# Two adaLN units weighed by GpSimd in attention in place of the even input stage, and the odd input stage's opening in another order

## Chip, cores and metric

One core of a Trainium2 chip runs the whole program. The time is device time in microseconds from the first to the last instruction of an execution, with what lies around it; lower is better. The engines are TensorE (PE; its weight loads are PEld), VectorE (DVE), ScalarE (ACT), GpSimd (POOL) and SyncE (SP), which issues most of the transfers.

## What is computed

A backbone of two layers over 512 latent tokens and 256 context tokens, all in float32, width 1024. Layer 0 mixes with a state-space scan beside an mLSTM, layer 1 with windowed and dense attention; each is followed by a mixture of experts. Each layer's normalised input is shifted and scaled, and each result gated, by six vectors of 1024 numbers (adaLN), once for the latent tokens (from `c`) and once for the context (from `c_ctx`):

```python
def adaln(cond, w, b):
    m = cond @ w + b
    return [t[:, None, :] for t in jnp.split(m, 6, axis=-1)]

sh1, sc1, g1, sh2, sc2, g2 = adaln(silu_c, ada_w[layer], ada_b[layer])
csh1, csc1, cg1, csh2, csc2, cg2 = adaln(silu_cc, ada_w[layer], ada_b[layer])
```

`ada_w` is 2 x 1024 x 6144, 48 MB in all. In the last layer the context is read by attention only, so of its context vectors only the first two (`csh1`, `csc1`) are used.

## The kernel before

The program is a row of blocks, one for each stage; at the end of a block all engines meet. In order: front, even input stage (`phase_in_even`), recurrent stage, output stage 0, experts 0, odd input stage (`phase_in_odd`), attention (`phase_attention`), output stage 1, experts 1 with the last stage. Within a block each engine runs its own list of instructions in order, and semaphores join the lists.

**The adaLN product** is cut into six units of 2048 columns (1024 rows, eight tiles of 128 x 2048, 1 MB each). Unit 0 is done in the front. `ADA_ORDER` names the other five, counted from unit 1. Its first two (units 1 and 2, the rest of layer 0) are the *direct* ones: `direct(k, v)` (line 790) multiplies on PE, with the condition columns `kit.ccol` as 32 columns of weights and four pieces of 128 x 512 as moving data, into four column groups of one bank. Tile k of both is loaded by SP (line 663) and multiplied in pair q = k + 2, one group of four products after `p7`, one after `p2`. The last three (units 4, 5 and 3) go another way: DVE's `weigh` (line 1120 and 1124) scales a 1 MB tile by its column and adds it up, for both conditions, in 24 slots spread over the z blocks, and PE sums over the partitions (`sum_ada`).

**The even input stage** computes a 768 x 1024 by 1024 x 5680 product. Its first 2560 columns come as ten pairs of 128 columns (q = 0 to 9), then six z blocks of 512. Each pair is a 2 x 2 product by seven half-size products, `p1` to `p7`, in the order p1, p6, p7, p4, p2, p5, p3 on PE. GpSimd makes the sums of weights `s1` to `s4` (lines 891, 892, 893, 898) and, between s4 and s2, stores turned tiles (`store_tokens`, line 861). `p6(q)` needs `s2(q)`. DVE evicts and adds the products (`u2` 1042, `u3` 1052, `c21` 1063, `c11` 1069, `c22_u4` 1075 and 1076, `c12` 1082), applies the convolution (`taps`, 1092), evicts the turned tiles of pair q - 2 (`to_tokens`, 1106, twice in a pair: behind `u3` and behind `c11`) and does one step of the gates' arithmetic in each pair, behind `c21`.

**The odd stage's opening.** At the end of experts 0, DVE combines tile 0's two expert rows (lines 2855 and 2857), evicts the last expert product (`give`, 2822), and then adds. SP's `load_odd` loads the first 2 MB of the layer's weights there, `load_odd_later` (line 3013 too) the other 4 MB at the start of the odd block. GpSimd gathers expert rows of tiles 1 and 2 (`gather_rows`, 3025, two gathers of 512 KB for a tile). ACT normalises tile 0, scales tile 1's row (3208) when its gathers are there, and only then takes its half of tile 0's turned columns (`take_x(0)`, 3229), for which PE's first product waits.

**Attention** runs over 32 groups g (4 query tiles x 2 kinds x 4 heads in pairs). PE's order is scores(g + 2), `turn(g)` (transposes of the weights p into the three banks `ps_t`, taken out by ACT and DVE in turn), at some g the turning and spreading of the reciprocals, and a quarter of the value product of the four groups before (`weigh`). SP loads the output weights (16 transfers, line 3473) and the router's (82). GpSimd copies one small tile (3480) and has nothing else.

## Time and profile before

| | us |
|---|---|
| median of 3 runs (lowest, highest) | 1650.42 (1648.29, 1650.96) |
| the profiled execution | 1649.59 |
| its span | 1647.8 |
| mean granted clock of TensorE, share of full | 0.950 |
| PE busy in the span | 1466.6 |
| DVE / ACT / POOL busy | 894.7 / 464.6 / 295.2 |
| bytes moved by DMA | 355.07 MB |

The page gives one execution. Busy time says which engine has no room; a wait says what an engine's next instruction was held by; a timeline gives the order. Times in the rows are microseconds from the span's start. The pairs lie from about 54 to 267 us, the z blocks behind them to about 480, the odd stage from 1092 to 1222, attention from 1222 to 1380.

### The profile page before, as it was taken

What the parts mean: (1) busy time and instruction counts of PE and PEld (TensorE: products, weight loads), DVE (VectorE), ACT (ScalarE), POOL (GpSimd) and SP (SyncE); (2) the same over time, 40 slices, a digit from 0 to 9 for tenths busy, and PEclk for the clock granted to TensorE, in tenths of its full rate; (3) what the DMA queues carried; (4) which work ended last, traced back from release to release, by engine and by line L of the source; (5) the groups of instructions that cost most, each with busy time, mean ns of one, the idle gap of its engine ahead of it and who ended that gap; (6) DMA issues with size and microseconds to landing.
All of it is one profiled execution on the core that took longest, in us unless ns stands there. A gap on an engine that the chain in (4) does not pass through costs nothing. (4 is left out here: it accounts for less than half of the span.)

```text
span 1647.8 us, 19901 instructions
## 1 busy us (share of the span) xinstructions
PE 1466.6 (89%) x7530; PEld 843.1 (51%) x7530; DVE 894.7 (54%) x1492; ACT 464.6 (28%) x957; POOL 295.2 (18%) x273
## 2 busy tenths in 40 slices
PE   4999999999997999799994999759989999949894
PEld 2555556888886777444541334324445554423331
DVE  4659978877674667355316211135567663453125
ACT  4132113100118677322101111124226662110001
POOL 1233222010004775321101000021000001010001
PEclk9999999999997999899996999979989999979997
DMA  9577784656576998734325999573021004659974
GB/s 343 193 222 223 244 262 148 252 199 219 201 222 205 301 272 246 286 139 156 112 90 213 391 378 407 224 278 130 13 67 38 2 1 154 255 216 401 419 330 166
DMA packets 173087, 355.07 MB, mean 215 GB/s; under 512 B 17809, under 2 KB 108257, under 8 KB 156225
## 3 DMA queue, kind: packets, MB, share of 16 engines
q1 hardware_dynamic: 151432, 278.31, 48.7%
q0 software_dynamic: 16288, 58.12, 9.3%
q10 hardware_dynamic: 5273, 17.38, 2.7%
q8 instruction: 60, 0.98, 0.2%
q14 instruction: 34, 0.28, 0.1%
HBM read 297.72 MB, written 56.05 MB: 215 GB/s over the span
## 5 line engine op out<-in xcount | busy, mean ns | idle before, releaser
L2660 PE MATMUL ex_ps_gu<-room,ex_xT 128*32 128x512 f32 x1472 | 170.6, 615 | 10.5 <-DMA room<-in_moe_w_up_dram 5.5
L2060 PE MATMUL po_ps_y<-room,po_yT 128*128 128x512 f32 x320 | 139.4, 593 | 2.0 <-DVE po_n L1957 2.0
L738 PE MATMUL ie_pq<-room,aT_even 128*128 128x256 f32 x576 | 127.6, 379 | 0.0
L738 PEld LDWEIGHTS ie_pq<-room,aT_even 128*128 128x128 f32 x576 | 109.2, 190 | 16.6 <-issue 1.7
L2660 PEld LDWEIGHTS ex_ps_gu<-room,ex_xT 128*32 128x32 f32 x1472 | 57.1, 113 | 116.5 <-issue 111.3
L734 PE MATMUL ie_pq<-aT_even,room 128*128 128x384 f32 x320 | 108.3, 486 | 0.0
L2811 DVE TENSOR_TENSOR ex_hid<-ex_hid,ex_ps_gu 128x256 f32<-128x256 f32 x25 | 10.5, 421 | 164.5 <-ACT ex_hid L2758 164.5
L2060 PEld LDWEIGHTS po_ps_y<-room,po_yT 128*128 128x128 f32 x320 | 60.0, 190 | 74.0 <-issue 71.7
L2685 PE MATMUL ex_ps_d<-room,ex_hT 128*32 128x512 f32 x736 | 83.7, 594 | 4.7 <-DVE ex_hT L2815 3.2
L734 PEld LDWEIGHTS ie_pq<-aT_even,room 128*128 128x128 f32 x320 | 59.7, 190 | 38.5
L2758 ACT ACTIVATE ex_hid<-ex_ps_gu 128x256 f32<-128x256 f32 x25 | 9.6, 384 | 218.1 <-PE ex_ps_gu L2660 193.1
L2521 POOL DMA_INDIRECT ex_xg<-t,slots_in x25 | 24.0, 961 | 232.3 <-PE ex_ps_x L2636 197.2
L738 PE MATMUL ie_pq<-room,ie_mixed 128*128 128x256 f32 x288 | 64.4, 379 | 0.0
L1439 ACT ACTIVATE room<-room,tokS 128x128 f32<-128x128 f32 x192 | 57.4, 388 | 19.4 <-DMA room<-ac_rows 19.4
L738 PEld LDWEIGHTS ie_pq<-room,ie_mixed 128*128 128x128 f32 x288 | 54.6, 190 | 8.2 <-issue 0.8
L1957 DVE TENSOR_TENSOR po_n<-po_ps_y,po_gate 128x512 f32<-128x512 f32 x20 | 13.7, 687 | 80.2 <-PE po_ps_y L2060 63.4
L3590 ACT ACTIVATE room<-room,io_ya 128x768 f32<-128x768 f32 (+2 forms) x64 | 54.7, 855 | 8.9 <-DVE io_ya L3643 7.9
L734 PE MATMUL ie_pq<-ie_mixed,room 128*128 128x384 f32 x160 | 56.5, 496 | 0.0
L3158 PE MATMUL io_ps_w<-room,io_aT 128*128 128x512 f32 x128 | 56.1, 592 | 0.0
L3513 PE MATMUL at_ps_s<-room 64*128 64x256 f32 (+2 forms) x288 | 47.8, 458 | 7.9 <-DVE io_ya L3640 7.1
L3154 PE MATMUL io_ps_w<-room,io_aT 128*128 128x512 f32 x96 | 45.1, 623 | 8.0 <-ACT io_aT L3229 8.0
L1537 PE MATMUL rc_ps_a<-rc_xdt,room 128*128 128x64 f32 x384 | 47.6, 286 | 4.8 <-DVE room L1583 4.8
(568 smaller groups left out, 2666.5 us busy)
## 6 DMA issues: line engine op xcount, KB each, us to landing
room<-in_moe_w_gate_dram SPq DMA_DIRECT2D x33, 1024.0 KB, 8.6
room<-in_moe_w_up_dram SPq DMA_DIRECT2D x33, 1024.0 KB, 12.3
room<-in_moe_w_down_dram SPq DMA_DIRECT2D x33, 1024.0 KB, 11.7
room<-in_ada_w_dram SPq DMA_DIRECT2D x29, 1024.0 KB, 5.2
room<-in_ev_w_in_dram SPq DMA_DIRECT2D x6, 2048.0 KB, 9.0
room<-ac_rows SPq DMA_DIRECT2D x12, 1024.0 KB, 6.6
y<-ex_y ACTq DMA_DIRECT2D x24, 512.0 KB, 8.6
room<-in_ev_w_in_dram SPq DMA_DIRECT2D x10, 1024.0 KB, 6.2
```

The lines of the kernel that those rows point to most:

```text
L734: ins = nc.tensor.matmul(to, w[:, k, :], x[:, k, :], start=(k == 0), stop=(k == KH - 1))
L738: ins = nc.tensor.matmul(to[:, T * 2 * P:(T + 1) * 2 * P], x[:, k, T * P:(T + 1) * P], w[:, k, :], start=(k == 0), stop=(k == KH - 1))
L1439: last = ACTV(mt[d][:, h, :], mt[d][:, h, :], ACT.Relu, scale=-1.0, bias=kit.tokS[:, T, 32 + 16 * d + h:33 + 16 * d + h])
L1537: last = MM(ps_a[:, h * SSD_P:(h + 1) * SSD_P], mt[d][:, h, :], xdt[d][:, h, :], start=True, stop=True)
L2060: last = nc.tensor.matmul(ps_y[:, c * BANK:(c + 1) * BANK], yT[n % 2][:, k, :] if even else kit.oT[:, k, n * P:(n + 1) * P], (w[:, k] if e ...
L2521: pool.indirect_dma_start(out=kit.xg[s][:, :], out_offset=None, in_=kit.t, in_offset=bass.IndirectOffsetOnAxis(ap=kit.slots_in[:, c:c + 1] ...
L2660: last = MM(ps_gu[s][rows, :, :], xT[s][:, k, rows], wgu[slot[q]][:, :, k, :], start=(k == 0), stop=(k == KD - 1))
L2685: last = MM(ps_d[rows, h * BANK:(h + 1) * BANK], hT[s][:, k, rows], wd[slot[q]][:, k, h * BANK:(h + 1) * BANK], start=(k == 0), stop=(k == ...
L3154: last = MM(ps_kv(T)[:, :].rearrange("p (a n) -> p a n", a=2), lhsT, w[:, k, :].rearrange("p (a n) -> p a n", a=2)[:, :, 512:768], start=( ...
L3158: last = MM(ps_w[c][:, :], lhsT, w[:, k, at:at + 512], start=(k == 0), stop=(k == KD - 1))
L3513: last = MM(ps_s[u][:, a:b], qT[rows, i, kind * 4 + j, :], key[rows, :], start=True, stop=True)
L3590: ACTV(sc[g % RING][u][:, 0:n], sc[g % RING][u][:, 0:n], ACT.Exp, scale=SCALE, bias=neg[:, b % 2, head:head + 1], accum_out=rsum[:, b % 2, ...
```

## The change

- Units 1, 2 and 3 now go through `weigh` in the z blocks' 24 slots; the direct products, their 64 loads and their waits are gone. Four bias loads and four stores of rows go too. A copy of `kit.ccol`'s first columns is put beside it (`image_col`).
- Units 4 and 5 (the last 4096 columns of layer 1, for the latent tokens alone) are computed in attention, as eight units of 512 columns: SP loads 64 tiles of 128 x 512 through three buffers behind the output weights; GpSimd scales each in place by its column (the first of a unit into the sum) and adds; at groups 7, 10, ..., 28 PE sums over the partitions with a column of ones (`sum_mod`), into a fourth kind of use of the three banks, and DVE adds the row to the bias (`take_mod`). SP stores the rows at the end.
- At the end of experts 0 DVE's `give` stands ahead of tile 0's combination. At the odd stage's opening SP's `load_odd_later` and GpSimd's gather of tile 2 wait for tile 1's gathers, and ACT takes tile 0 before it scales tile 1.

```diff
@@ -93,6 +93,7 @@
         self.mcol = self.keep("mcol", [P, 2, DEPTH, 2, KD])
         self.scale1 = self.keep("scale1", [P, 2, DEPTH, KD])
         self.ccol = self.keep("ccol", [P, KD, 32])
+        self.image_col = self.ccol[:, KD - 1, 32 - KD:32]
...
-    ADA_ORDER = (0, 1, 3, 4, 2)
-    DIRECT = 2
-    ADA_SLOTS = (len(ADA_ORDER) - DIRECT) * KD
+    ADA_HERE = 3
+    ADA_SLOTS = ADA_HERE * KD
...
@@ -652,18 +647,9 @@
...
-                for v in range(DIRECT):
-                    if q > 2:
-
-                        sp.wait_ge(direct_read[v], q - 2)
-                    elif v:
-                        sp.wait_ge(tail_ready, 1)
-                    rows = ada_rows(v, q - 2)
-                    for j in range(4):
-                        sp.dma_start(direct_w[v][j], rows[:, j * BANK:(j + 1) * BANK]).then_inc(direct_loaded[v], 16)
 
...
-            sp.wait_ge(ada_taken, len(ADA_ORDER))
+            sp.wait_ge(ada_taken, ADA_HERE)
...
-            def direct(k, v):
-
-                pe.wait_ge(direct_loaded[v], 64 * (k + 1))
-                for j in range(4):
-                    last = nc.tensor.matmul(direct_acc[v][32 * j:32 * j + 32, :], kit.ccol[:, k, :], direct_w[v][j], start=(k == 0), stop=(k == KD - 1))
-                last.then_inc(direct_read[v], 1)
...
-            SUMS = {(PAIRS + 1, 5, 2): 2, (PAIRS + 3, 5, 2): 3, (LAST, 5, 0): 4}
...
-                if 2 <= q < PAIRS:
-                    direct(q - 2, 0)
                 p4(q)
                 if 2 <= q < PAIRS:
                     turn(q - 2, 1)
                 p2(q)
-                if 2 <= q < PAIRS:
-                    direct(q - 2, 1)
...
+            V.tensor_copy(kit.image_col, kit.ccol[:, :, 0])
...
                     next(steps)
...
                 if q == PAIRS + 2:
+                    take_row(0)
+                if q == PAIRS + 4:
+                    take_row(1)
+                if q == LAST:
                     take_row(2)
-                if q == PAIRS + 4:
-                    take_row(3)
-                if q == LAST:
-                    take_row(4)
...
@@ -2850,12 +2812,12 @@
             else:
                 ch = kit.route_chain
                 x0, ya0, yb0, gate0 = kit.cx[0][:, :], kit.cya[0][:, :], kit.cyb[0][:, :], kit.cgate[0][:, :]
+                give(n + (NP - 1), LB, held[LB] * 16)
                 dve.wait_ge(kit.cy_loaded[0], 32)
                 dve.wait_ge(late_taken, 2)
                 ch(V.scalar_tensor_tensor(ya0, yb0, kit.wts[:, 0, 1:2], ya0, ALU.mult, ALU.add))
                 dve.wait_ge(kit.gate_loaded, 32)
                 ch(V.tensor_tensor(ya0, ya0, gate0, ALU.mult))
-                give(n + (NP - 1), LB, held[LB] * 16)
                 dve.wait_ge(kit.cx_loaded[0], 16)
...
 
         @block.sync
         def _(sp):
-            sp.wait_ge(y_loaded[0], 32)
+            sp.wait_ge(y_loaded[1], 32)
             kit.load_odd_later(sp)
...
-            for n in range(1, RING):
-                gather(n)
+            gather(1)
+            pool.wait_ge(y_loaded[1], 32)
+            gather(2)
             pool.wait_ge(kit.small_loaded, 64)
...
             norm(0)
+            take_x(0)
             scale_first(1)
-            take_x(0)
             norm(1)
...
+        AW, ACOLS = 3, 2 * D
+        ada_w, ada_sum = kit.ada_w, [kit.ada_sum, kit.cyb[0][:, BANK:2 * BANK]]
+        ada_rows, one_col = kit.cyb[0][32:64, 0:BANK], kit.one_col
         mx, neg, rsum, snk, es, rec = (kit.cya[0][:, BANK + 16 * n:BANK + 16 * n + 16].rearrange("p (b h) -> p b h", h=8) for n in range(6))
         rec_t, rec_b = kit.cyb[0][0:8, 0:P], kit.cya[0][:, 0:BANK]
         ps_s = [ps(f"ps_s{u}", [P, 2 * BANK]) for u in range(2)]
@@ -3443,6 +3409,10 @@
             S(n) for n in ("sel_ready", "s_ready", "largest", "neg_ready", "p_ready", "snk_ready", "es_ready"))
         t_ready, t_act, t_dve, rec_ready, o_ready, o_taken, chain_v = (
             S(n) for n in ("t_ready", "t_act", "t_dve", "rec_ready", "o_ready", "o_taken", "chain_v"))
+        ada_loaded = [S(f"ada_loaded{j}") for j in range(AW)]
+        ada_step, ada_scaled, bias_loaded, col_ready, rows_stored = (
+            S(n) for n in ("ada_step", "ada_scaled", "bias_loaded", "col_ready", "rows_stored"))
+        MODS = {7 + 3 * r: r for r in range(2 * KD // 2)}
...
+            if g in MODS:
+                use("dve", ("mod", MODS[g]))
...
+            sp.dma_start(ada_rows[0:KD, :], A["ada_b"][1, ACOLS:ACOLS + KD * BANK].rearrange("(r x) -> r x", x=BANK)).then_inc(bias_loaded, 16)
             load_router(kit, sp, 1)
+            for m in range(KD * KD):
+                r, k = m // KD, m % KD
+                if m >= AW:
+                    sp.wait_ge(ada_step, m - AW + 1)
+                sp.dma_start(ada_w[m % AW], A["ada_w"][1][k * P:(k + 1) * P, ACOLS + r * BANK:ACOLS + (r + 1) * BANK]).then_inc(ada_loaded[m % AW], 16)
+            sp.wait_ge(t_dve, taken_at["mod", KD - 1][1])
+            sp.dma_start(kit.mod[0, 6 * D + ACOLS:6 * D + ACOLS + KD * BANK].rearrange("(r x) -> r x", x=BANK), ada_rows[0:KD, :]).then_inc(rows_stored, 16)
+            sp.wait_ge(rows_stored, 16)
 
         @block.gpsimd
         def _(pool):
             kit.retire("ex0_")
             G = nc.gpsimd
+            G.memset(one_col[:, :], 0.0).then_inc(col_ready, 1)
+            pool.wait_ge(col_ready, 1)
+            G.memset(one_col[:, 31:32], 1.0).then_inc(col_ready, 1)
             G.tensor_copy(sel[:, :, :, :], consts[0:8, 0:8].rearrange("k (u j) -> k j u", j=4).unsqueeze(3).to_broadcast([8, 4, 2, HD])).then_inc(sel_ready, 1)
+            def scale(m):
+                r, k = m // KD, m % KD
+                pool.wait_ge(ada_loaded[m % AW], m // AW * 16 + 16)
+                if k == 0 and r >= 2:
+                    pool.wait_ge(t_dve, taken_at["mod", r - 2][1])
+                to = ada_w[m % AW] if k else ada_sum[r % 2]
+                G.tensor_scalar(to, ada_w[m % AW], kit.image_col[:, k:k + 1], None, ALU.mult).then_inc(ada_scaled if k else ada_step, 1)
+
+            scale(0)
+            for m in range(KD * KD):
+                r, k = m // KD, m % KD
+                if k < KD - 1:
+                    scale(m + 1)
+                if k:
+                    pool.wait_ge(ada_scaled, r * (KD - 1) + k)
+                    pool.wait_ge(ada_step, m)
+                    G.tensor_tensor(ada_sum[r % 2], ada_sum[r % 2], ada_w[m % AW], ALU.add).then_inc(ada_step, 1)
+                if k == KD - 1 and r < KD - 1:
+                    scale(m + 1)
 
         @block.tensor
         def _(pe):
@@ -3546,6 +3549,13 @@
                 pe.wait_ge(rec_ready, b + 1)
                 TR(bank[0:8, 0:P], rec[:, b % 2, :], consts[:, 0:P]).then_inc(t_ready, 1)
 
+            def sum_mod(r):
+                pe.wait_ge(ada_step, KD * (r + 1))
+                if r == 0:
+                    pe.wait_ge(col_ready, 2)
+                bank = slot(("mod", r))
+                MM(bank[32:64, :], one_col[:, 31 - r:63 - r], ada_sum[r % 2], start=True, stop=True).then_inc(t_ready, 1)
+
             def spread_rec(b):
                 wait_taken(("rec", b))
                 if b == 0:
...
@@ -3567,6 +3577,9 @@
                         turn_rec(b)
                     if q == 2:
                         spread_rec(b)
+                if g in MODS:
+                    sum_mod(MODS[g])
+                if b >= 0:
                     weigh(b, share(b, q))
             turn_rec(NB - 1)
             for q in range(4):
@@ -3666,6 +3679,15 @@
                 what = ("rec", b)
                 dve.wait_ge(t_ready, place[what] + 1)
                 V.tensor_copy(rec_t[:, :], ps_t[place[what] % 3][0:8, 0:P]).then_inc(t_dve, 1)
+
+            def take_mod(r):
+                what = ("mod", r)
+                dve.wait_ge(t_ready, place[what] + 1)
+                if r:
+                    dve.wait_ge(t_dve, taken_at["mod", r - 1][1])
+                else:
+                    dve.wait_ge(bias_loaded, 16)
+                TT(ada_rows, ada_rows, ps_t[place[what] % 3][32:64, :], ALU.add).then_inc(t_dve, 1)
 
             def give(b):
                 i, kind = b // 2, b % 2
@@ -3690,6 +3712,8 @@
                         take_rec(b)
                     if q == 3:
                         give(b)
+                if g in MODS:
+                    take_mod(MODS[g])
             invert(NB - 1)
             take_rec(NB - 1)
             give(NB - 1)
@@ -3750,6 +3774,9 @@
             kit.kT = low[:, NT * QKV:NT * QKV + 2 * TOK].rearrange("p (a n) -> p a n", a=2)
             kit.qT = high[:, 0:(NT - CT) * D].rearrange("p (i k q) -> p i k q", k=KD, q=P)
             kit.odd_spare = high[:, (NT - CT) * D:SLOT]
+            kit.ada_w = [low[:, NT * QKV + 2 * TOK + j * BANK:NT * QKV + 2 * TOK + (j + 1) * BANK] for j in range(3)]
+            kit.ada_sum = rest[:, (KD - 5) * D:(KD - 5) * D + BANK]
+            kit.one_col = kit.odd_spare[:, TOK + 9 * P:TOK + 9 * P + 64]
             kit.masks = kit.odd_spare[:, 0:TOK], kit.odd_spare[:, TOK:TOK + 5 * P], kit.odd_spare[:, TOK + 5 * P:TOK + 9 * P]
             phase_in_odd(kit)
             phase_attention(kit)
```

## Rows read from the trace of the kernel before

**Rows 1.** busy time (instructions) of PE, PEld, DVE, ACT, POOL; PEclk, DMA share, GB/s

```profile
91.00:267.00 176.00, 171.05 (x652) 92.71 (x651) 140.19 (x180) 40.85 (x48) 53.87 (x40) 1.00 0.71 227
1092.00:1106.00 14.00, 2.11 (x9) 1.74 (x10) 3.16 (x8) 5.04 (x9) 8.98 (x14) 0.50 0.90 343
1096.00:1098.00 2.00, 1.82 (x8) 1.42 (x8) 0.14 (x1) 0.00 (x0) 1.69 (x3) 0.50 1.06 411
1122.00:1126.00 4.00, 4.00 (x12) 2.50 (x13) 2.78 (x10) 2.92 (x7) 1.87 (x2) 0.57 0.61 151
1244.00:1245.00 1.00, 0.89 (x7) 0.41 (x4) 0.96 (x4) 0.86 (x3) 0.00 (x0) 1.00 0.03 3
1250.00:1370.00 120.00, 117.83 (x725) 65.96 (x723) 80.67 (x234) 75.28 (x168) 0.00 (x0) 1.00 0.00 1
```

**Rows 2.** waits of PE, 55 to 262 us: total, times, longest us

```profile
PE ie_pq L734 <- POOL ie_mixed_w L898: 4.9, 4, 2.7
```

**Rows 3.** timeline of PE, pairs: start, us, operation, count [idle <-releaser]

```profile
158.81 2.85 PE L734 MATMUL ie_pq<-ie_mixed,ie_mixed_w 128*128 128x384 f32 x8 [1.34 <-POOL ie_mixed_w L898]
...
164.82 1.06 PE L794 MATMUL ie_pq<-ie_late,ccol 128*32 128x512 f32 x8
...
165.82 2.85 PE L734 MATMUL ie_pq<-ie_mixed,room 128*128 128x384 f32 x8
...
180.68 2.85 PE L734 MATMUL ie_pq<-ie_mixed,ie_mixed_w 128*128 128x384 f32 x8
```

**Rows 4.** timeline of DVE, pair 5

```profile
155.36 0.95 DVE L1106 COPY xzo<-ie_pq 128x768 f32<-128x768 f32 x1
...
168.71 0.55 DVE L1063 TENSOR_TENSOR room<-room,ie_pq 128x384 f32<-128x384 f32 x1 [1.63 <-PE ie_pq L734]
```

**Rows 5.** timeline of POOL, pairs 5 and 6

```profile
156.61 0.84 POOL L861 DMA_DIRECT2D tokc<-xzo  x1 [6.58 <-DVE xzo L1106]
157.47 1.28 POOL L898 TENSOR_TENSOR ie_mixed_w<-room 128x512 f32<-128x512 f32 x1
...
179.34 1.29 POOL L898 TENSOR_TENSOR ie_mixed_w<-room 128x512 f32<-128x512 f32 x1
```

**Rows 6.** timeline, opening of the odd stage, and landing of the gathers (L3025)

```profile
1082.65 0.59 ACT L2766 COPY ex_y<-ex_ps_d 128x512 f32<-128x512 f32 x1 [1.27 <-PE ex_ps_d L2685]
...
1084.06 0.69 DVE L2822 COPY ex_y<-ex_ps_d 128x512 f32<-128x512 f32 x1
...
1094.54 0.94 POOL L3025 DMA_INDIRECT io_yb<-y,pos  x1 [0.30 <-issue]
...
1103.22 1.15 ACT L3208 ACTIVATE io_ya<-io_ya,wts 128x1024 f32<-128x1024 f32 x1 [7.42 <-DMA io_yb<-y,pos]
...
1121.94 1.61 PE L3133 MATMUL io_ps_x<-consts,io_yb 128*128 128x128 f32 x8 [2.65 <-ACT io_yb L3223]
...
DMA to landing us min/median/max: 4.2/6.5/10.2
```

**Rows 7.** SP's 64 direct loads (L663), 256 KB each: time to landing

```profile
DMA to landing us min/median/max: 2.8/3.7/6.9
```

**Rows 8.** groups of POOL: out<-in xcount | busy, mean ns | idle before

```profile
L893 POOL TENSOR_TENSOR room<-room,ie_mixed_w 128x512 f32<-128x512 f32 x10 | 15.5, 1546 | 75.9 <-PE ie_pq L734 75.9
...
L1351 POOL TENSOR_TENSOR room<-room 128x512 f32<-128x512 f32 x10 | 12.7, 1274 | 1.8 <-DMA room<-w_rows 1.8
...
L3102 POOL COPY io_wn<-io_wn_row 128x512 f32<-128x512 f32 x1 | 0.6, 617 | 0.0
```

**Rows 9.** attention: turning of groups 7, 28 (PE); end of SP's issues; last DVE

```profile
1261.20 1.66 PE L3523 MATMUL at_ps_t<-consts,room 128*128 128x128 f32 x12
...
1357.42 1.67 PE L3523 MATMUL at_ps_t<-consts,room 128*128 128x128 f32 x12
...
1233.54 3.46 SPq L82 DMA_DIRECT2D wr<-in_moe_w_expert_dram  x1
...
1379.50 0.69 DVE L3674 TENSOR_TENSOR room<-at_ps_o,io_ya 128x512 f32<-128x512 f32 x1 [6.83 <-ACT io_ya L3610]
```

More of the change, by code:

```diff
@@ L407, in phase_in_even @@
         mixed_w = sb("mixed_w", [P, KH * 2 * P])
-        direct_w = [[late[:, j * BANK:(j + 1) * BANK] for j in range(4)],
-                    [kit.tokS[:, :, :].rearrange("p t c -> p (t c)")[:, 0:BANK], kit.tokM[:, :, :].rearrange("p t c -> p (t c)")[:, 0:BANK],
-                     w_tail[:, :, :].rearrange("p k n -> p (k n)")[:, 0:BANK], mixed_w[:, KH * P:KH * 2 * P]]]
         pq = st.enter_context(nc.psum_tensor("ie_pq", [P, 8 * BANK], F32))
@@ L420, in phase_in_even @@
         ada_sum = [tok_flat[:, 0:ADA_W], kit.ada_acc1]
-        ada_row = [feat[v // 3][:, :, :].rearrange("p t n -> p (t n)")[:, v % 3 * BANK:(v % 3 + 1) * BANK] for v in range(ADA_UNITS - 1)]
+        ada_row = [feat[0][:, :, :].rearrange("p t n -> p (t n)")[:, v * BANK:(v + 1) * BANK] for v in range(ADA_HERE)]
         ada_acc = pq[:, 7 * BANK:8 * BANK]
-        direct_acc = [ada_acc, pq[:, 6 * BANK:7 * BANK]]
         half = [[aT[:, i * KH:(i + 1) * KH, j * TH:(j + 1) * TH] for j in range(2)] for i in range(2)]
@@ L433, in phase_in_even @@
         ada_loaded, ada_step = [S(f"ada_loaded{s}") for s in range(3)], S("ada_step")
-        direct_loaded, direct_read = [S(f"direct_loaded{v}") for v in range(DIRECT)], [S(f"direct_read{v}") for v in range(DIRECT)]
         ada_summed, ada_taken = S("ada_summed"), S("ada_taken")
@@ L633, in ada_rows @@
         def ada_rows(v, k):
-            unit = ADA_ORDER[v] + 1
+            unit = v + 1
             cols = unit % (ADA_UNITS // DEPTH) * ADA_W
@@ L682, in _ @@
                 sp.wait_ge(feat_stored[h], times_stored(STORED, PAIRS - 2 + h))
-                n = 3 - h
-                for j in range(4):
-                    sp.dma_start(feat[h][32 * j:32 * j + 2, :, :].rearrange("p t n -> p (t n)")[:, 0:n * BANK].rearrange("p (u x) -> p u x", u=n),
-                                 bias_view[j][1 + 3 * h:1 + 3 * h + n, :].partition_broadcast(2)).then_inc(bias_loaded, 16)
+            for j in range(4):
+                sp.dma_start(feat[0][32 * j:32 * j + 2, :, :].rearrange("p t n -> p (t n)")[:, 0:ADA_HERE * BANK].rearrange("p (u x) -> p u x", u=ADA_HERE),
+                             bias_view[j][1:1 + ADA_HERE, :].partition_broadcast(2)).then_inc(bias_loaded, 16)
             Z_AT = {4: 2, 8: 3, 12: 4, 16: 5}
@@ L788, in turn @@
                 last.then_inc(turned, 1)
[L790 to L795 removed]
             def sum_ada(v):
[L799 to L800 removed]
+                pe.wait_ge(ada_step, 2 * KD * (v + 1))
+                if v == 0:
                     pe.wait_ge(keep_clear, 2)
[L802 removed]
+                else:
+                    pe.wait_ge(ada_taken, v)
                 for cond in range(2):
@@ L831, in _ @@
                     last.then_inc(packM_turned, 1)
-                    pe.wait_ge(ada_taken, len(ADA_ORDER))
+                    pe.wait_ge(ada_taken, ADA_HERE)
                     for s in range(4):
@@ L1127, in take_row @@
             def take_row(v):
-                if v < DIRECT:
-                    dve.wait_ge(direct_read[v], KD)
-                else:
-                    dve.wait_ge(ada_summed, v - DIRECT + 1)
-                dve.wait_ge(bias_loaded, 128)
-                row = ada_row[ADA_ORDER[v]]
-                TT(row, direct_acc[v] if v < DIRECT else ada_acc, row, ALU.add).then_inc(ada_taken, 1)
+                dve.wait_ge(ada_summed, v + 1)
+                dve.wait_ge(bias_loaded, 64)
+                TT(ada_row[v], ada_acc, ada_row[v], ALU.add).then_inc(ada_taken, 1)
             steps = gates(dve, V, ch)
```

25 lines of the change are left out of this document (7 added, 18 removed).

## The prediction

> **What bounds the kernel now.** I read the page's first part (its busy times stand in the table), then the busy time by stretches, then the waits and the timelines of the three places that the change touches. TensorE (PE) is busy for most of the span, so what counts is where it has no idle time. The pairs of the even input stage are such a place (171.05 of 176.00 us at full clock) and attention too (117.83 of 120.00 us) [rows 1]. The opening of the odd input stage is not: of 14 us PE works 2.11, at half clock, while the DMA engines are 90% busy [rows 1]. In the pairs PE's only idle time is 4.9 us in four waits for GpSimd's L898 [rows 2]. In attention GpSimd does nothing (0.00 us) and hardly any data move (1 GB/s) [rows 1]; the change uses both.
>
> **Part 1, the direct products leave the pairs: -11 us.** Pairs 2 to 9 each hold two groups of eight records at L794, 16 groups. One group costs the distance to the next start: 164.82 to 165.82, 1.00 us [rows 3]. At most 16.0 us go. They don't all come back, for another loop is nearly as long as PE's: VectorE (DVE) takes c21, does a step of the gates, evicts the second turned tile (L1106, its end at 156.31), GpSimd stores it (156.61, 0.84) and only then makes s2 (157.47, 1.28), for which p6 waits until 158.81; p6, turning, p7, the first direct group and p4 follow, and DVE's next c21 starts at 168.71 [rows 3 to 5]. The group behind p7 lies on this loop, so its 1.00 us is saved in all eight pairs: 8.0. The group behind p2 lies beside it. It counts only where the next p6 was not released by s2: the four waits of rows 2 (next pairs 4, 5, 7, 9) and next pair 6, where s2 ended at 180.63 and p6 began at 180.68, make five pairs in which it only turns into waiting [rows 2, 3, 5]. Three are left: 3.0. Together -11.0 us; the bounds are -8 (DVE, idle for only 1.63 us before that c21 [rows 4], has no room) and -16. 64 loads of 256 KB leave the SP queue there; the wait that they could shorten is the load before L892, which no PE wait of rows 2 names: nothing. The three units left in the input stage keep DVE's 24 slots, so the z blocks keep their length. The copy of eight columns, four bias and four row DMAs fewer, and two row additions fewer on DVE I put at nothing: each lies beside PE's full stretch; uncovered it would be some tenths.
>
> **Part 2, the odd stage's opening: -5 us.** (a) DVE's last eviction of the experts (L2822) starts at 1084.06, behind L2857, though its input was there at 1082.65, when ScalarE (ACT) took its half [rows 6]. Moved ahead of the wait it starts 1.4 us sooner, and PE's L2746 and the last y store with it. The block ends with that store's landing, in which 2 MB of weights share the DMA engines, so I count 1.0 (0.3 to 1.4). (b) The second gather of tile 1 is issued at 1094.54, and ACT, which waits for it ahead of its half of tile 0, gets it at 1103.22, 8.7 us later [rows 6]. From 1096 on the engines carry 411 GB/s [rows 1]: the second group of weight columns, 4 MB, was issued just ahead. The change puts those, and the gather of tile 2, behind tile 1's landing. Other gathers of this kernel landed in 4.2 us at the least [rows 6], so the data come at about 1099: 4.2 sooner. From there a chain of ACT and DVE leads to the turning of tile 2 (PE at 1121.94, after 2.65 us idle) [rows 6] and it moves as a whole; I count 4.0 (bounds 1 and 7). The price: weight columns 0 to 511 start 4 us later and are wanted at 1128; 4 MB at 411 GB/s are 10 us, so they land by 1112. Tile 2's gather is late by 3 us; before, ACT went on to it without idle time, so a part of the gain may be lost there. That is inside the bounds.
>
> **Part 3, attention: +31.5 us.** Eight units of 8 tiles (128x512): GpSimd scales each tile by its column and adds seven of them up; PE sums over the partitions into a row (2 records, like one column group of L794 alone: a group of four took 1.00 us, so I take 1.0, bounds 0.4 and 1.2); DVE adds the row (0.7 us, in its idle time). PE's eight products are 8.0 us of the 120 that had no room. But PE also waits in its own order: `sum_mod(r)` stands behind `turn(7 + 3r)`, and scores, turning and weighing queue behind it. PE wants unit 0 at 1262.8 and unit 7 at 1359.0 [rows 9] (the ends of the two turnings), one unit in 13.75 us, 14.7 with the product.
> What can GpSimd deliver? An addition of 128x512 took 1.273 us; a copy, one input like the scaling, 0.617 [rows 8]. The trace has no scaling on GpSimd: the bounds are the copy (below it nothing was seen) and the addition, and I take 0.62, being nearer in form. With 0.05 for the semaphores of the two (in rows 5 the gap between two operations is 0.02) a tile is 1.94 us of work, a unit 8 x 0.64 + 7 x 1.29 = 14.2. That alone would nearly do. But the tiles come through three buffers. Tile m is loaded when addition m-3 is done; until GpSimd wants it there is one scaling and one addition, 1.94 us. A load of 256 KB of the same matrix took at least 2.8 us from issue to landing (median 3.7 of 64, four of them always issued together) [rows 7]; with 0.15 for SP to see the semaphore and GpSimd to start, 2.95. So GpSimd waits for every tile. Two tiles take max(2 x 1.94, 2.95 + 1.94) = 4.9 us, one 2.45, eight 19.6; at a unit's start there is no addition and the buffer is given back at once, which saves 1.6: 18.0 us per unit, against the 14.7 that PE allows. Worked through tile by tile in the same way, a landing in 2.3 us would make it 16.5, in 2.0 15.6, in 1.5 14.7.
> First data: SP issues the output weights and the router's until 1237.0 [rows 9]; the DMA engines are quiet from 1244 on [rows 1], so the first tile is there at 1244.5, unit 0 is done 17.3 later at 1261.8, in time, unit 7 at 1261.8 + 7 x 18.0 = 1387.8. Behind it stand the product (1.0) and what PE did between 1359.0 and the end of the stage, 1380.2 [rows 9]: 21.2. Each wait will be 3 to 4 us, and after the 2.65 us of idle before 1121.94 PE's clock was 0.57 for the next 4 us [rows 1, 6], for most of them the lower of its two levels (1.2 of 2.4 GHz): 1.9 us more behind the last wait. Attention then ends at 1387.8 + 1.0 + 21.2 + 1.9 = 1411.9 instead of 1380.2: +31.7, taken as 31.5. The row's store (16 KB, SP) and its landing lie beside those 21 us.
>
> What contention with DVE adds I read from L893, the same addition beside DVE's taps: 1.546 on the mean [rows 8]. Beside attention's DVE work, which takes one operand from PSUM, I keep 1.27; 1.52 would add about 10 us (a unit of 19.2 us). The Trainium skill (SBUF — State Buffer, Who interferes with whom) says that a DVE instruction with at most one SBUF input doesn't contend with GpSimd; by that the price stays at 1.27. The trace agrees with its other half, that two SBUF inputs do contend: L893's 1.546.
>
> **Sum.** -11.0 - 5.0 + 31.5 = +15.5. The profiled execution took 1649.59 us, which gives 1665.1; the median of the runs is 0.83 above it, so I say 1666.
>
> **Rivals.** (A) The ring keeps up: a load comes back in 1.5 us or less from the freed buffer, a unit costs GpSimd at most 14.7 us, and PE never waits; only the 8 products remain. -16 + 8 = -8: 1642, faster. For it: GpSimd's bare work fits the spacing of three groups. Against it: 64 loads of this matrix and shape, none below 2.8. (B) In a quiet queue the loads land in 2.0 to 2.3 us: a unit takes 15.6 to 16.5, attention +13 to +20, sum -3 to +4: 1648 to 1655. The kernel becomes slower from a landing of 2.1 us on. (C) The scaling costs what a two-input operation costs (1.27): a tile is 2.6 us, a unit 20.6, attention +53, sum +37: 1687. (D) The pairs give all 16 and the opening 7: 1659, inside the forecast's case.
>
> **Chances.** Forecast (with D; 1656 to 1676) 0.55, A 0.17, B 0.13, C 0.15 (with milder forms of it from 1676 on). The range goes from A's value to most of C's: 1643 to 1686. A measurement of this kernel can tell about 0.2%, 3.3 us, from no change. Slower: 0.55 + 0.15 + a little of B = 0.72; same 0.07; faster: A and the lower part of B, 0.21.
>
> **What would show it.** Right: PE waits for GpSimd at the product of each unit, 3 to 4 us each from unit 1 on; GpSimd's idle time there ends with the loads of ada_w; its scaling near 0.62 us; L898 still ahead of p6 in five pairs; stage of the pairs 11 us shorter; tile 1 at about 1099 on the old scale. Wrong: loads landing under 2.2 us; a scaling of over 1 us; no PE wait in attention at all; or a pairs stage that is shorter by 8 or by 16.

## The result, and the profile after

The kernel after takes 1692.9 us (median of four runs, 1686.3 to 1697.1) where the kernel before takes 1649.4 (1640.0 to 1651.0): ratio 1.0276 with an interval of 1.0249 to 1.0304, slower by some 44 us. The forecast was 1666 with a range of 1643 to 1686: the sign was right, the size was not.

The profiled executions have spans of 1647.8 and 1694.6 us, 46.8 apart. By stages, from the first instruction of each on PE:

| | before | after | difference | forecast |
|---|---|---|---|---|
| up to the first p6 that is compared (91 us) | 91.1 | 91.2 | +0.1 | 0 |
| pairs, to the first product of the z blocks | 176.3 | 168.1 | -8.2 | -11 |
| z blocks to ACT's last eviction of experts 0 | 815.2 | 815.8 | +0.5 | 0 |
| from there to attention | 140.1 | 134.6 | -5.5 | -5 |
| attention | 157.8 | 222.6 | +64.8 | +31.5 |
| output stage 1 to the end | 267.2 | 262.3 | -5.0 | 0 |

The last line is no work of the change: the same stages took between 258.1 and 265.6 us in eight profiles of the kernels below in which they compute the same, and the 267.2 of before lies just above these. The table compares one execution of each kernel. How far a stage moves without any edit in it, experiments 1 and 8 show: the pairs of before took 178.0 us in two other profiles, and attention as in the kernel after took 219.8 us in another one. The case is decided in attention.

Busy time by stretches of the kernel after (columns as in [rows 1]): first the pairs, then attention.

```profile
91.21:259.33 168.12, 157.41 (x526) 93.97 (x524) 141.57 (x180) 40.76 (x48) 53.80 (x40) 0.97 0.47 151
...
1210.00:1432.00 222.00, 170.96 (x880) 85.25 (x879) 107.55 (x296) 92.07 (x205) 169.47 (x123) 0.85 0.36 96
```

In [rows 1] both stages had PE with hardly any idle time. Now attention has 51 us of it, with a granted clock of 0.85, and GpSimd is busy for 169 of the 222 us. The waits of PE (us in total, times, longest), of the pairs and of attention, name the engine:

```profile
PE ie_pq L717 <- POOL ie_mixed_w L869: 10.7, 5, 3.8
...
PE at_ps_t L3557 <- POOL room L3481: 21.6, 4, 7.6
PE at_ps_t L3557 <- POOL io_yb L3481: 17.7, 4, 4.6
```

L3557 is the product of `sum_mod`, L3481 GpSimd's addition: all eight products wait, 39.3 us in all. The timeline shows the spacing (start, duration; the first, second and eighth product, then PE's next stage) and with it the start of GpSimd's work:

```profile
1209.73 1.65 PE L3516 MATMUL at_ps_s<-room 64*128 64x256 f32 x6 [0.86 <-PEq L3000]
...
1233.47 4.67 POOL L3471 TENSOR_SCALAR room<-room,ccol 128x512 f32<-128x512 f32 x3 [21.88 <-DMA room<-in_ada_w_dram]
...
1255.59 1.91 PE L3557 MATMUL at_ps_t<-room 128*32 128x512 f32 x2 [5.87 <-POOL room L3481]
...
1277.03 1.92 PE L3557 MATMUL at_ps_t<-io_yb,room 128*32 128x512 f32 x2 [4.64 <-POOL io_yb L3481]
...
1407.23 1.92 PE L3557 MATMUL at_ps_t<-io_yb,room 128*32 128x512 f32 x2 [4.14 <-POOL io_yb L3481]
...
1432.34 1.19 PE L2022 MATMUL po_ps_y<-io_x,room 128*128 128x512 f32 x2 [1.81 <-PEq L3391]
```

(1407.23 - 1255.59) / 7 = 21.66 us a unit, against the forecast's 18.0. Why is in GpSimd's groups (count | busy us, mean ns | idle before, released by):

```profile
L3471 POOL TENSOR_SCALAR room<-room,ccol 128x512 f32<-128x512 f32 x60 | 93.7, 1565 | 25.8 <-DMA room<-in_ada_w_dram 24.6
```

The scaling takes 1565 ns. The forecast took it as 620, and its upper bound was 1270, the addition. It said that the trace of before has no scaling on GpSimd. There is one, in the recurrent stage, written in another form (a two-input multiplication, the column broadcast along the row), at 1039 ns:

```profile
L1371 POOL TENSOR_TENSOR rc_kw<-room,tokM 128x512 f32<-128x512 f32 x10 | 10.4, 1039 | 0.0
```

The page's part on DMA has the loads (count, size, us to landing):

```profile
room<-in_ada_w_dram SPq DMA_DIRECT2D x64, 256.0 KB, 2.8
```

They land in 2.8 us, as the forecast had it. Of GpSimd's 24.6 us of waiting for them, 21.88 lie before the first tile (the timeline above): only 2.7 us are left in which the ring of three buffers held it up. The additions kept their 1.27 us (1268 and 1270 ns for the two destinations) beside DVE's attention work. That agrees with what the Trainium skill says (SBUF — State Buffer, Who interferes with whom) of DVE instructions with at most one SBUF input, outside its two-port modes: they do not contend with GpSimd.

### The profile page after: what moved, and what is told of

It reads as the page before. It is cut to its first block and busy times, and to the rows that moved or that the text cites. A ratio compares the mean times of both kernels' runs of the same rounds, so it can differ in the third digit from the quotient of the medians.

```text
span 1694.6 us, 19886 instructions
## 1 busy us (share of the span) xinstructions
PE 1480.3 (87%) x7418; PEld 850.4 (50%) x7418; DVE 903.8 (53%) x1499; ACT 464.4 (27%) x957; POOL 466.2 (28%) x395
## 5 line engine op out<-in xcount | busy, mean ns | idle before, releaser
L721 PEld LDWEIGHTS ie_pq<-room,aT_even 128*128 128x128 f32 x576 | 109.2, 190 | 16.6 <-issue 1.7
L3471 POOL TENSOR_SCALAR room<-room,ccol 128x512 f32<-128x512 f32 x60 | 93.7, 1565 | 25.8 <-DMA room<-in_ada_w_dram 24.6
L2773 DVE TENSOR_TENSOR ex_hid<-ex_hid,ex_ps_gu 128x256 f32<-128x256 f32 x25 | 10.5, 421 | 161.6 <-ACT ex_hid L2720 161.6
L3516 PE MATMUL at_ps_s<-room 64*128 64x256 f32 (+2 forms) x288 | 51.4, 485 | 7.9 <-DVE io_ya L3653 7.0
L3615 ACT COPY at_pT<-at_ps_t 128x384 f32<-128x384 f32 (+1 forms) x64 | 29.0, 452 | 102.3 <-PE at_ps_t L3526 101.3
L3121 PE MATMUL io_ps_w<-room,io_aT 128*128 128x512 f32 x128 | 56.1, 592 | 0.0
```

The lines of the kernel that those rows point to most:

```text
L721: ins = nc.tensor.matmul(to[:, T * 2 * P:(T + 1) * 2 * P], x[:, k, T * P:(T + 1) * P], w[:, k, :], start=(k == 0), stop=(k == KH - 1))
L3121: last = MM(ps_w[c][:, :], lhsT, w[:, k, at:at + 512], start=(k == 0), stop=(k == KD - 1))
L3471: G.tensor_scalar(to, ada_w[m % AW], kit.image_col[:, k:k + 1], None, ALU.mult).then_inc(ada_scaled if k else ada_step, 1)
L3516: last = MM(ps_s[u][:, a:b], qT[rows, i, kind * 4 + j, :], key[rows, :], start=True, stop=True)
L3615: nc.scalar.copy(pT[g // 4 % 2][u][:, 0:len(tiles), j, :], ps_t[place[what] % 3][:, 0:len(tiles) * P].rearrange("p (t q) -> p t q", q=P)). ...
```

## Experiments

Two of the kernels leave out or change a part of the computation, and say which. Attention's length is always taken from the first scores to the first product of the output stage on PE; without the units it took 157.7 to 158.5 us in four profiles, where whole times vary by some us.

**1. The opening alone.** The kernel before with part 2 of the change only.

```diff
+                give(n + (NP - 1), LB, held[LB] * 16)
                 dve.wait_ge(kit.cy_loaded[0], 32)
...
-            sp.wait_ge(y_loaded[0], 32)
+            sp.wait_ge(y_loaded[1], 32)
...
-            for n in range(1, RING):
-                gather(n)
+            gather(1)
+            pool.wait_ge(y_loaded[1], 32)
+            gather(2)
...
-            scale_first(1)
             take_x(0)
+            scale_first(1)
```

> The kernel before with part 2 alone (the odd stage's opening and the eviction ahead of the combination). Theory (the parts of the change are separate, the opening gives 5.5 us as read between the two traces): 5.5 us under before, attention beginning 5.5 us sooner. Rival (the trace's 5.5 us came from run to run differences of the experts and the gathers): within 2 us of before.

Measured: 1641.7 us against 1646.3, ratio 0.9963 (0.9944 to 0.9982), and on another chip, beside experiment 9, the same kernel again:

> The kernel before with the opening alone in its new order, a second time, on the chip of e10, so that the two can be compared: ratio 0.996 again. By the theory e10 is 2 to 4 us below it (8 us less in the pairs, 6 us more in attention); by the rival 2 us above.

1642.1 us against 1647.0, ratio 0.9967 (0.9949 to 0.9985). Both are gains of some 5 us, in line with the forecast's -5. In the kernel after the same edit shows where they come from (opening, the rows that answer to [rows 6]):

```profile
1075.10 0.59 ACT L2728 COPY ex_y<-ex_ps_d 128x512 f32<-128x512 f32 x1 [1.20 <-PE ex_ps_d L2647]
1075.10 0.69 DVE L2784 COPY ex_y<-ex_ps_d 128x512 f32<-128x512 f32 x1 [4.05 <-PE ex_ps_d L2647]
...
1085.50 0.93 POOL L2987 DMA_INDIRECT io_yb<-y,pos  x1 [0.30 <-issue]
...
1090.67 1.15 ACT L3171 ACTIVATE io_ya<-io_ya,wts 128x1024 f32<-128x1024 f32 x1 [0.35 <-DMA io_yb<-y,pos]
...
1110.55 1.10 PE L3096 MATMUL io_ps_x<-consts,io_yb 128*128 128x128 f32 x8 [2.05 <-ACT io_yb L3186]
```

DVE's eviction starts with ACT's instead of 1.4 us behind it. The second gather of tile 1 reaches ACT 5.2 us after its issue (1085.50 to 1090.67) instead of 8.7, which saves 3.5. From ACT's last eviction to tile 2's turning it was 39.3 us before (1082.65 to 1121.94) and is 35.5 now, 3.8 less; the other 1.7 of the stage's 5.5 us come right behind it, where PE ran tile 2's turning and its first product in 4.4 us (granted clock 1.00) instead of 6.1 (0.72).

**2. The kernel after without attention's units.** It leaves the last 4096 columns of layer 1's vectors at their bias.

```diff
-        MODS = {7 + 3 * r: r for r in range(2 * KD // 2)}
+        MODS = {}
...
```

The loads of the tiles and GpSimd's work on them go too.

> The changed kernel without the eight units in attention: no tiles, no work of GpSimd, no product and no row addition (the last two vectors of layer 1 are then not computed). Theory (pairs -8, opening -5.5, all of the loss in attention): 13.5 us under before, attention 158 us long as before, pairs' stage as in the changed kernel. Rival (the input stage and what follows it also lose something to the change): less than 10 under before.

Measured: 1706.4 us, ratio 1.0354 (1.0323 to 1.0385), which no theory expected. By stages it is as expected as far as the vectors are not yet used: attention took 157.7 us (before 157.8). So all of the 64.8 us come from the units. The output stage and experts 1 took 337 us instead of 262. With other vectors the last router sends tokens elsewhere: the branch for experts that hold more tokens runs for more of them, with 64 records of this product where the same stretch of the kernel after has 16. First the kernel after, then this one:

```profile
L2660 PE MATMUL ex_ps_gu<-room,ex_xT 128*128 128x512 f32 x16 | 7.1, 599 | 0.0
```

```profile
L2660 PE MATMUL ex_ps_gu<-room,ex_xT 128*128 128x512 f32 x64 | 34.1, 694 | 27.5 <-DMA room<-in_moe_w_up_dram 27.5
```

A kernel that leaves out something on which routing depends can be read stage by stage only.

**3. Scaling in another form.** The product with the column goes through the two-input operation, the column broadcast along the row.

```diff
-                G.tensor_scalar(to, ada_w[m % AW], kit.image_col[:, k:k + 1], None, ALU.mult)
+                G.tensor_tensor(to, ada_w[m % AW], kit.image_col[:, k:k + 1].to_broadcast([P, BANK]), ALU.mult)
```

> The changed kernel, GpSimd's scaling written as a multiplication of two tensors with the column broadcast (1.04 us for that form in the recurrent stage of before, against 1.57 for the scaling by a per-partition scalar). Theory (the scaling's price is the term that was mis-sized, and the ring of three is next in line at a landing of 2.8 us): a unit takes 19.4 us instead of 21.7, in all 18 us less than the changed kernel. Rival 1 (the ring doesn't count): own work 17.2 us a unit, 34 us less. Rival 2 (any multiplication by a column costs 1.57 in attention): no difference.

Measured: 1672.7 us, ratio 1.0153 (1.0115 to 1.0191), 20 us below the kernel after. The same arithmetic costs 1040 ns:

```profile
L3471 POOL TENSOR_TENSOR room<-room,ccol 128x512 f32<-128x512 f32 x60 | 62.4, 1040 | 39.0 <-DMA room<-in_ada_w_dram 38.5
```

That is the price of L1371 in the trace of before. Attention took 199.2 us, a unit 19.3. Idle time for loads rose from 24.6 to 38.5 us, although the loads are the same: with GpSimd faster, the ring binds.

**4. And five buffers.**

```diff
-        AW, ACOLS = 3, 2 * D
-        ada_w, ada_sum = kit.ada_w, ...
+        AW, ACOLS = 5, 2 * D
+        ada_w, ada_sum = kit.ada_w + [proj[:, j, 0:BANK] for j in range(2)], ...
```

> The kernel of e3_broadcast with five buffers instead of three (two in columns of proj that attention doesn't read). Theory (both terms): a unit takes 17.2 us, 34 us less than the changed kernel, 16 less than e3. Rival (the ring doesn't count): equal to e3.

Measured: 1656.4 us, ratio 1.0055 (1.0030 to 1.0080). Attention took 181.4 us, a unit 16.9, which is 8 x 1.00 + 7 x 1.235, the distances of GpSimd's starts, with 0.3 over. What is left of waiting is that before the first tile:

```profile
L3471 POOL TENSOR_TENSOR room<-room,ccol 128x512 f32<-128x512 f32 x60 | 61.8, 1038 | 21.7 <-DMA room<-in_ada_w_dram 21.7
```

**5. Five buffers alone**, with the scaling of the kernel after.

> The kernel after with five buffers in place of three for attention's ada_w tiles, nothing else. Theory (GpSimd's own work binds: a unit is 8 x 1.565 + 7 x 1.27 = 21.4 us of work, and its idle time for loads behind the first was 2.7 us in all): 1 to 4 us less than the kernel after, attention 219 to 222 us. Rival (the ring of three buffers binds, as the prediction said): attention about 18 us shorter, as from e3 to e4, where the scaling was cheap.

Measured: 1690.3 us, ratio 1.0244 (1.0201 to 1.0287); attention 218.3 us, a unit 21.2. That is 4.3 us less than in the kernel after and 1.5 less than in experiment 8, whose attention is the same code and took 219.8 us. So the ring of three costs 1.5 to 4.3 us there, about what was expected, but 17.8 once the scaling is cheap (experiments 3 and 4). Two bounds lie close together here, and the larger hid the other.

**6. Which part of the scaling costs.** A constant in place of the column, so the last 4096 columns hold other values and the experts behind attention get other tokens, as in experiment 2.

```diff
-                G.tensor_scalar(to, ada_w[m % AW], kit.image_col[:, k:k + 1], None, ALU.mult)
+                G.tensor_scalar(to, ada_w[m % AW], 0.5, None, ALU.mult)
```

> The kernel after, with GpSimd's scaling by the constant 0.5 in place of the column of the condition, so the last 4096 columns of layer 1's vectors come out wrong and what follows attention is not to be compared. Price of the form: the column cost 1565 ns for 128x512, the product with a broadcast column 1040 ns, the copy 617 ns. Theory 1 (reading the scalar from memory is what costs): about 0.6 to 1.0 us, attention 180 to 205 us. Theory 2 (GpSimd's tensor-by-scalar operation costs that in any form): 1.5 to 1.57 us, attention 222 us as in the kernel after.

```profile
L3471 POOL TENSOR_SCALAR room<-room 128x512 f32<-128x512 f32 x60 | 89.2, 1488 | 25.0 <-DMA room<-in_ada_w_dram 23.5
```

1488 ns: reading the scalar is worth 77 ns, the operation itself is slow. That is just below theory 2's 1.5 to 1.57 and far above theory 1's. In the one execution attention took 214.3 us, where theory 2 said 222; the whole time (1706.2 us) is not to be compared.

**7. The tiles sooner.** Experiment 4, and SP issues the tiles ahead of the output weights and the router's, which it slips in between.

```diff
+                if AW <= m < AW + 2 * KD:
+                    o, u = divmod(m - AW, 2)
+                    sp.dma_start(kit.ow[o][u * HD:(u + 1) * HD, :], w_view[o // 4, o % 4, u]).then_inc(kit.ow_loaded[o], 16)
+                if m == AW + 2 * KD:
+                    load_router(kit, sp, 1)
```

> The kernel of e4 (scaling by a broadcast column, five buffers), and SP issues attention's ada_w loads first, the 16 output weight loads between them and the router's behind them. In e4 GpSimd's first scaling began 23.6 us after attention's start, since its first tile is queued behind the other loads, and a unit took it 16.8 us, against the 14.7 that PE allows; PE waited 9.0 us for it. Theory (late start and GpSimd's own work are what is left of the loss): first scaling 3 to 5 us after attention's start, so unit 7 is done some 20 us sooner, at about 138 us of the stage, ahead of PE, which wants it at about 142; no wait of PE for L3481, eight products of about 1.05 us are all that remains: attention 157.8 + 8.4 = 166 us (e4 181.4, after 222.6, before 157.8), the whole kernel about 5 us below the kernel before. Rival (PE is held by something else that the units bring, such as DMA traffic or DVE's rows): attention stays above 172 us with waits of PE on other semaphores.

Measured: 1640.9 us, ratio 0.9965 (0.9944 to 0.9986); attention 168.2 us. PE no longer waits for L3482, GpSimd's addition here; a product has no idle time but for DVE's eviction:

```profile
1213.52 3.03 POOL L3472 TENSOR_TENSOR room<-room,ccol 128x512 f32<-128x512 f32 x3 [1.53 <-DMA room<-in_ada_w_dram]
...
1265.98 1.05 PE L3558 MATMUL at_ps_t<-io_yb,room 128*32 128x512 f32 x2
...
1310.92 1.02 PE L3558 MATMUL at_ps_t<-room 128*32 128x512 f32 x2 [0.19 <-DVE at_pT L3670]
```

The first tile is scaled 20 us sooner. This is the kernel that the change was on the way to, and it is no better than the opening alone (experiment 1): attention, 10.4 us longer, takes back what the pairs gave (167.7 us against 178.0 in experiment 1), and 8.3 of these are the products.

**8. Filler in the pairs.** The kernel after, and in each pair 0.96 us of work for PE that nobody reads, where one of the removed groups stood.

```diff
                 p2(q)
+                if 2 <= q < PAIRS:
+                    for h in range(2):
+                        for j in range(4):
+                            nc.tensor.matmul(pq[32 * j:32 * j + 32, 6 * BANK + 224 * h:6 * BANK + 224 * h + 224], kit.ccol[:, q - 2, :], ...)
                 p5(q)
```

> The kernel after, with eight products of 128 x 32 by 224 columns behind p2 in pairs 2 to 9 (about 0.9 us of PE's time each pair), whose results nobody reads, in the place of one of the two removed groups. In the kernel after PE's waits for s2 grew to 1.86, 2.53, 1.02, 1.45 and 3.85 us, and three of the p6 behind them took 4.4 to 4.5 us instead of 2.85. Theory (this group only fills waiting time where s2 comes late, and PE's clock falls after longer idle time): the five waits shrink by about 0.9 each, one or two of the three slow p6 take 2.85 again, and the pairs end 1.5 us sooner to 1 us later than in the kernel after, although PE does 7 us more. Rival (the filler costs its time wherever it stands, or the slow p6 have another cause): the pairs end 3 to 7 us later and the slow p6 remain.

Here are p6 of pairs 4, 5 and 9 and the first product of the z blocks, in the kernel after:

```profile
131.99 4.54 PE L717 MATMUL ie_pq<-ie_mixed,ie_mixed_w 128*128 128x384 f32 x8 [1.86 <-POOL ie_mixed_w L869]
...
155.85 4.54 PE L717 MATMUL ie_pq<-ie_mixed,ie_mixed_w 128*128 128x384 f32 x8 [2.53 <-POOL ie_mixed_w L869]
...
242.17 4.42 PE L717 MATMUL ie_pq<-ie_mixed,ie_mixed_w 128*128 128x384 f32 x8 [3.85 <-POOL ie_mixed_w L869]
...
259.33 2.97 PE L721 MATMUL ie_pq<-room,aT_even 128*128 128x256 f32 x13
```

and with the filler, whose own record stands second:

```profile
134.35 2.85 PE L717 MATMUL ie_pq<-ie_mixed,ie_mixed_w 128*128 128x384 f32 x8 [0.77 <-POOL ie_mixed_w L873]
146.18 0.96 PE L801 MATMUL ie_pq<-ccol 128*32 128x224 f32 x16
156.52 2.85 PE L717 MATMUL ie_pq<-ie_mixed,ie_mixed_w 128*128 128x384 f32 x8 [1.44 <-POOL ie_mixed_w L873]
...
242.25 4.19 PE L717 MATMUL ie_pq<-ie_mixed,ie_mixed_w 128*128 128x384 f32 x8 [2.76 <-POOL ie_mixed_w L873]
...
260.62 5.34 PE L721 MATMUL ie_pq<-room,aT_even 128*128 128x256 f32 x24
```

This execution, the only one, took 1690.7 us. It is 1.27 us late from its start (its first p6, of pair 2, begins at 92.48, the other's at 91.21). From there to the z blocks both take 168.1 us, with 7.7 us more work for PE in one. Two of three slow p6 are gone and the waits fell from 10.7 to 5.2 us. Experiment 3 has the same comparison without any edit in the pairs: there pair 4 waited 1.87 us too, but its p6 ran in 2.85 us.

```profile
133.57 2.85 PE L717 MATMUL ie_pq<-ie_mixed,ie_mixed_w 128*128 128x384 f32 x8 [1.87 <-POOL ie_mixed_w L869]
155.75 4.54 PE L717 MATMUL ie_pq<-ie_mixed,ie_mixed_w 128*128 128x384 f32 x8 [2.54 <-POOL ie_mixed_w L869]
```

From pair 4 to pair 5 it took 22.18 us, the kernel after 23.86: one slow p6 costs its whole 1.7 us, since it lies on the loop that sets the pairs' pace. (The stage as a whole was only 0.3 us shorter, 167.8: in that execution p6 of pair 9 took 5.49 us instead of 4.42.) The kernel before and experiment 1 show the same for pair 9, with the same code and the same wait; the stage took 176.3 us and 178.0:

```profile
249.44 2.85 PE L734 MATMUL ie_pq<-ie_mixed,ie_mixed_w 128*128 128x384 f32 x8 [2.66 <-POOL ie_mixed_w L898]
```

```profile
251.41 4.54 PE L734 MATMUL ie_pq<-ie_mixed,ie_mixed_w 128*128 128x384 f32 x8 [2.66 <-POOL ie_mixed_w L898]
```

The granted clock (column PEclk) during pair 4's p6 says why; first the kernel after, then experiment 3:

```profile
132.00:136.50 4.50, 4.50 (x10) 2.51 (x11) 3.90 (x4) 0.98 (x3) 2.75 (x2) 0.62 1.09 375
```

```profile
133.60:136.40 2.80, 2.80 (x10) 1.69 (x11) 2.73 (x3) 0.51 (x2) 2.49 (x2) 1.00 1.11 357
```

0.62 means the lower level (1.2 of 2.4 GHz) for most of it. After the same wait the clock fell in one execution and not in the other, so the wait makes it possible and not certain. Of the eight profiles of kernels with the pairs of the kernel after, p6 of pair 4 is slow in five and fast in three; p6 of pairs 5 and 9, behind 2.53 and 3.85 us, is slow in all eight.

**9. Fewer products.** Experiment 7 with four sums in place of two; PE sums two units at once, in two column groups.

```diff
-        MODS = {7 + 3 * r: r for r in range(2 * KD // 2)}
+        MODS = {7 + 3 * r: r for r in range(1, 2 * KD // 2, 2)}
...
-                MM(bank[32:64, :], one_col[:, 31 - r:63 - r], ada_sum[r % 2], start=True, stop=True).then_inc(t_ready, 1)
+                for i in range(2):
+                    last = MM(bank[32 + 32 * i:64 + 32 * i, :], one_col[:, 32 - r - i:64 - r - i], ada_sum[(r - 1 + i) % 4], start=True, stop=True)
+                last.then_inc(t_ready, 1)
```

> The kernel of e5 with four sums in place of two, and PE summing two units at once: four products instead of eight, each in two column groups, behind groups 10, 16, 22 and 28. In e5 attention took 168.2 us, 10.4 more than before, without a wait for GpSimd, and the eight products had 1.02 to 1.05 us each. The four records of a former direct group ran in 1.0 us, no longer than one column group alone. Theory (the products are what is left, and two column groups run side by side): four products of about 1.05 us, attention 163 to 165 us, the whole kernel some 4 us below e5, about 9 us below before (ratio 0.994). Rival (the two groups run one behind the other, or the 10 us have another source): products of 2 us, attention 168 us, as e5.

Measured: 1634.6 us (1629.8 to 1640.8), ratio 0.9916 (0.9893 to 0.9938): some 58 us below the kernel after and 7 below the opening alone on the same chip. In three of the four products, four records for two units take what two took for one:

```profile
1297.76 1.05 PE L3560 MATMUL at_ps_t<-room 128*32 128x512 f32 x4
```

The first product took 1.6 us, at a granted clock of 0.63. Attention took 165.4 us, just above what was expected: 7.6 above before, of which the products are 4.7. The 2.9 us that are left are not settled; PE's waits for DVE's evictions there are longer by tenths only. The 7 us below the opening alone are also more than the 2 to 4 that were expected: in the two profiles the pairs are 10.5 us shorter and attention 7.7 longer, 2.8 in all, and where the rest comes from is not settled.

## Why the prediction was wrong

**The chain was right in kind.** PE waits for GpSimd at each unit's product, its whole list waits behind it, and attention runs at the pace of GpSimd's units; the z blocks kept their length. Attention's 33 us above the forecast are, term by term: the first tile 23.7 us after the stage's start instead of 21.7 (+2.0); unit 0 in 22.1 instead of 17.3 (+4.8); seven units at 21.66 instead of 18.0 (+25.6); behind the last product 25.1 instead of 24.1 (+1.0).

**The step that failed is the price of the scaling.** The prediction said that the trace had no row for it, bounded it by a copy (0.617) and an addition (1.274) [rows 8], and took the lower since a copy too has one tensor input. It measured 1.565, outside the bounds: the nearest row in form (inputs) was not the nearest in price. (A scaling of over 1 us was one of its signs of being wrong.) With 1.565 in place of 0.62 the forecast's own ring formula gives max(2 x 2.84, 2.95 + 2.84) = 5.8 us for two tiles, 23.2 for eight, less 1.6 is 21.6 a unit: what was measured. Its whole sum would then be about 1696 us (an estimate), against 1692.9, so this one price accounts for the miss. Rival C had the mechanism with 1.27 and gave 1687. The ring formula holds at another price as well: with 1.04 it gives 5.26 for two tiles and 19.4 a unit (experiment 3: 19.3), and the bare work without the ring is 16.6 to 17.2 (experiment 4: 16.9).

Two rows could have warned. The trace of before did hold a multiplication by a column on GpSimd, L1371 with 1.04, in a form that the change could have used; it would have given 19.4 us a unit beforehand. And the lower bound was one single instruction: the same copy took 0.91 to 0.93 us in the eleven other profiles. The Trainium skill (GPSIMD Engine Reference, 4.1 Engine selection) calls one-input operations of GpSimd roughly line-rate and sets only two-input ones apart as slower; for the scaling by a scalar the trace doesn't agree: it took longer (1.565) than the two-input addition (1.27), and the measurement decides.

**Bounds "from both sides" were not bounds.** Nothing excluded a price above the addition. A range reaching to twice the upper row would have held the time.

**Part 1, -8.2 instead of -11.** "Shorter by 8" was one of the prediction's own signs of being wrong. Three terms make up the 8.2. First, a direct group cost 1.19 us and not 1.00. Here are p6 of pairs 2 and 3, without a wait between them, before and after:

```profile
91.08 2.74 PE L734 MATMUL ie_pq<-ie_mixed,ie_mixed_w 128*128 128x384 f32 x8
112.84 2.74 PE L734 MATMUL ie_pq<-ie_mixed,ie_mixed_w 128*128 128x384 f32 x8
```

```profile
91.21 2.74 PE L717 MATMUL ie_pq<-ie_mixed,ie_mixed_w 128*128 128x384 f32 x8
110.59 2.74 PE L717 MATMUL ie_pq<-ie_mixed,ie_mixed_w 128*128 128x384 f32 x8
```

21.76 us became 19.38, so two groups were worth 2.38; the distance to the next start had left out that the products before and behind a group each took 0.1 us longer. Sixteen groups are 19.0 us. Second, the waits for s2 grew by 5.8 us (4.9 to 10.7). Third, three p6 behind them took 1.6 to 1.7 us more, 5.0 together. -19.0 + 5.8 + 5.0 = -8.2.

In the forecast's own split, the loop over DVE was right in kind: from the kernel before to experiment 8, in which of the two groups only the one behind p7 is gone without a stand-in, the pairs are 8.2 us shorter with one slow p6 (4.19 instead of 2.85), so 9.5 at equal clock, which is 8 x 1.19, where 8.0 was forecast. The group behind p2 gave nothing in the end, where 3.0 was forecast: at equal clock the kernel after would be at -13.2, with 3.7 from that group, but the slow p6 take 5.0 back. That a slow p6 costs its whole length is shown for pairs 4 and 9 and counted likewise for pair 5. The forecast had this price in attention (1.9 us behind the last wait) and left it out of the pairs. At which wait the clock falls could not be foretold, and stays open; against experiment 1's two profiles, whose p6 of pair 9 is slow already, the pairs are 9.9 us shorter.

**Part 2, -5.5 instead of -5.** The number was right, in part by luck. (a) gave 1.5, a little over its upper bound of 1.4: from ACT's last eviction to the issue of tile 1's second gather 11.9 us became 10.4. (b) gave 3.5 at the landing, but 2.3 at the turning of tile 2, where the forecast let the whole chain move by 4.0. Most of what was lost between the two is PE's turning of tile 1, which ran behind a wait at a granted clock of 0.50 and took 1.97 us (1.09 before), while ACT waited for it:

```profile
1099.06 1.97 PE L3096 MATMUL io_ps_x<-consts,io_yb 128*128 128x128 f32 x8 [2.55 <-ACT io_yb L3186]
```

The last 1.7 us are PE's higher clock behind tile 2's turning (experiment 1), which the forecast did not count. In experiment 1's two profiles the stage is 4.5 and 4.8 us shorter than before. The feared loss at tile 2's gather did not show: ACT went on to it without idle time.

**Rival A**, that the ring keeps up, needed a price that the kernel never came near to; its other half, the value of 1642 when PE never waits, is experiment 7 (1640.9).

## What to carry to other kernels

Before work goes to an idle engine, its form there needs a measured price: look through the whole trace for the same operation, and if it stands there in another form, write it in that form. Where no price is to be had, the bound is not the dearest neighbour in the trace, and the range must reach past it. Idle time that a stage without room offers to another engine is worth only what that engine's whole chain delivers per step (first data, ring, each operation), so work each of them out and fix them together: of the 65 us here, mended in this order, 23 were the operation's form, 18 the fourth and fifth buffer, 13 the order of SP's queue, and 10 were left with nothing to wait for, 8 of them the products. Mended alone, the buffers gave 1.5 to 4.3. And work taken from an engine that then waits may be worth nothing, since the wait can lower its clock for the work behind it.

## What the runs showed of the hardware that was not expected

- GpSimd multiplies 128 x 512 float32 by a column in 1565 ns as tensor by scalar, by a constant in 1488 ns, and by the same column broadcast in a two-input operation in 1040 ns; a two-input addition with two full inputs takes 1270 ns. One copy took 617 ns in the kernel before and 907 to 925 in the other profiles.
- PE's eight records behind a wait for GpSimd took 2.85 us or 4.2 to 5.5. By the length of the wait: behind 1.46 us and less always the short time; behind 1.87 us the short one in three profiles and the long one in five; behind 2.53 us the long one in eight of eight; behind 2.66 us the short one in one and the long one in two; behind 2.76 us the long one in one, behind 3.85 us in eight of eight. A product of two records took 1.05 us at the upper of PE's two clock levels (granted clock 1.00, 2.4 GHz) and 1.91 at the lower (0.50, 1.2 GHz).
- Two products of 128 x 512 in two column groups run in 1.05 us together, at the upper level; one alone takes the same.
